# Centering the values before a chunked recurrence instead of centering its outputs

## The reference, cut to what matters

```
state = state * w + (state @ -kk) (kk * a)^T + v k^T
y_t   = state @ r_t                       # one output per feature of v
mean  = mean(y over the head's 64 features);  var = mean((y - mean)^2)
y     = (y - mean) * rsqrt(var + eps) * gn_w + gn_b
y     = y + sum(r * k * r_k) * v          # the bonus, with v as it came
out   = (y * g) @ w_o
```

## Time and profile before

| | |
|---|---|
| runs | 2466.2, 2463.61, 2459.58 us |
| span of the profiled execution, first to last instruction | 2460.2 us |
| PE, DVE, ACT, POOL busy over the span | 2353.0, 1536.6, 663.3, 480.0 us |
| granted TensorE clock, mean | 0.980 |
| recurrence stage | about 557 to 873 us |

### The profile page before, as it was taken

The page is one execution under the profiler, slowest core; times in us unless marked ns, Lnnn a source line. Parts: engine busy times, 40 slices in busy tenths (PEclk is TensorE's granted clock), DMA queues, the critical chain, the costliest instruction groups (busy, mean ns, idle before and its releaser), DMA issues. The chain is left out here.

```text
span 2460.2 us, 43846 instructions
## 1 busy us (share of the span) xinstructions
PE 2353.0 (96%) x17560; PEld 1924.7 (78%) x17560; DVE 1536.6 (62%) x2155; ACT 663.3 (27%) x1274; POOL 480.0 (20%) x313
## 2 busy tenths in 40 slices
PE   7999998997988899999999999999999999999999
PEld 5888886784666678888888888888778887888887
DVE  6656567845777756556576564647766665655654
ACT  3101015535556531010023310102544552200001
POOL 3202131001111133121230221213221112212211
PEclk9999999998999999999999999999988999999999
DMA  4333333431010033333265243333300003233322
GB/s 140 99 89 102 95 94 90 143 112 58 30 30 27 4 103 94 104 93 103 77 197 141 84 121 93 97 92 100 80 1 14 15 1 92 85 106 90 105 83 73
DMA packets 371393, 206.53 MB, mean 84 GB/s; under 512 B 18400, under 2 KB 360352, under 8 KB 371232
## 3 DMA queue, kind: packets, MB, share of 16 engines
q1 hardware_dynamic: 364752, 192.11, 27.5%
q10 hardware_dynamic: 6480, 12.13, 1.4%
HBM read 192.61 MB, written 11.60 MB: 83 GB/s over the span
## 5 line engine op out<-in xcount | busy, mean ns | idle before, releaser
L162 PE MATMUL bank_b<-hhi_b,w_hi_b 128*128 128x512 f32 x872 | 345.6, 396 | 0.0
L164 PE MATMUL bank_b<-hhi_b,w_lo_b 128*128 128x512 f32 x872 | 339.5, 389 | 0.0
L163 PE MATMUL bank_b<-hlo_b,w_hi_b 128*128 128x512 f32 x872 | 339.3, 389 | 0.0
L151 DVE TENSOR_TENSOR w_lo_b<-w_raw,w_hi_b 128x1024 fp32r<-128x1024 f32 (+1 forms) x162 | 287.8, 1776 | 5.6
L162 PE MATMUL bank_a<-hhi_a,w_hi_a 128*128 128x512 f32 x480 | 188.7, 393 | 7.8 <-DVE hlo_a L582 7.8
L163 PEld LDWEIGHTS bank_b<-hlo_b,w_hi_b 128*128 128x128 f32 x872 | 163.7, 188 | 36.8 <-issue 3.4
L162 PEld LDWEIGHTS bank_b<-hhi_b,w_hi_b 128*128 128x128 f32 x872 | 163.7, 188 | 36.6 <-issue 3.4
L164 PEld LDWEIGHTS bank_b<-hhi_b,w_lo_b 128*128 128x128 f32 x872 | 163.7, 188 | 34.5
L163 PE MATMUL bank_a<-hlo_a,w_hi_a 128*128 128x512 f32 x480 | 187.8, 391 | 0.0
L164 PE MATMUL bank_a<-hhi_a,w_lo_a 128*128 128x512 f32 x480 | 187.5, 391 | 0.0
L467 ACT ACTIVATE gated_b<-gsc_b 128x512 f32<-128x512 f32 x44 | 27.9, 634 | 495.2 <-DVE gsc_b L378 495.1
(11 more groups left out here) (404 smaller groups left out, 4918.7 us busy)
## 6 DMA issues: line engine op xcount, KB each, us to landing
w_raw<-in_ffn_w_gate_dram SPq DMA_DIRECT2D x88, 512.0 KB, 3.9
w_raw<-in_ffn_w_up_dram SPq DMA_DIRECT2D x88, 512.0 KB, 3.9
w_raw<-in_ffn_w_down_dram SPq DMA_DIRECT2D x64, 512.0 KB, 3.8
w_raw<-in_ffn_w_down_dram SPq DMA_DIRECT2D x32, 384.0 KB, 3.2
w_raw<-in_rw_w_rkv_dram SPq DMA_DIRECT2D x24, 512.0 KB, 3.7
w_raw<-in_kv_w_dram SPq DMA_DIRECT2D x12, 512.0 KB, 4.7
w_raw<-in_rw_w_o_dram SPq DMA_DIRECT2D x8, 512.0 KB, 6.1
w_raw<-in_nsa_w_q_dram SPq DMA_DIRECT2D x8, 512.0 KB, 3.8
```

The lines of the kernel that those rows point to most:

```text
L151: nc.vector.tensor_tensor(lo, raw, fp(hi), ALU.subtract).then_inc(s["w_ready"], 1)
L162: nc.tensor.matmul(out, whi, hi, start=first, stop=False)
L163: nc.tensor.matmul(out, whi, lo, start=False, stop=False)
L164: return nc.tensor.matmul(out, wlo, hi, start=False, stop=last)
```

## The change

The matrix `center` moves to the front. `values(p)` multiplies v by `center` while turning it, so that `vtok` holds centered values and every output comes out centered. The product `centered` on PE and the copy to `dev` on ACT go. The squares are taken from `ysb` in SBUF, and the normalization reads `ysb`. Since `ysb` now lives until the normalization, it has three buffers (of the same total size as the two `dev` rows and the one `ysb` before), and its writer waits for the normalization three pairs earlier. For pair 0, `values` waits for the constants. The variance no longer waits for the copy.

```diff
@@ buffers
-        ysb, sqy = core.sq[:, 0], [core.sq[:, 1], row("sqy")[:]]
+        ysb, sqy = [core.sq[:, 0], row("ysb1")[:], row("ysb2")[:]], [core.sq[:, 1], row("sqy")[:]]
-        dev, yn = [row(f"dev{n}") for n in range(2)], row("yn")
+        yn = row("yn")
@@ PE
             def values(p):
                 at(pe, p, "lv", 16)
                 at(pe, p - 1, "tok", 3)
+                if p == 0:
+                    pe.wait_ge(s["consts"], 80)
                 for t in range(NT):
-                    m = nc.tensor.transpose(bank[:, TB, t * P:(t + 1) * P], v[:, t * P:(t + 1) * P], core.ident[:])
+                    m = mm(bank[:, TB, t * P:(t + 1) * P], v[:, t * P:(t + 1) * P], center[:], start=True, stop=True)
...
             def variance(p):
                 if 0 <= p < ND:
                     at(pe, p, "sqy", 1)
-                    at(pe, p, "dev", 1)
...
-            def centered(p):
-                if 0 <= p < ND:
-                    at(pe, p, "yadd", 1)
-                    mm(bank[:, EB], center[:], ysb, start=True, stop=True).then_inc(s["cen"], 1)
...
                 m.then_inc(s["f_mm"], 1)
-                centered(p - 1)
                 at(pe, p + 1, "vtok", 1)
...
             output_part(0, 1)
-            centered(last)
             output_part(1, 0)
@@ ACT
-                A(by_parity(ysb), parity_banks(slice(DB, TB + 1), HALF), ACT.Copy).then_inc(s["ysb"], 1)
+                at(act, p - 3, "yn", 1)
+                A(by_parity(ysb[p % 3]), parity_banks(slice(DB, TB + 1), HALF), ACT.Copy).then_inc(s["ysb"], 1)
             def squares(p):
                 if 0 <= p < ND:
-                    at(act, p, "cen", 1)
+                    at(act, p, "yadd", 1)
                     at(act, p - 2, "yn", 1)
-                    A(sqy[p % 2], bank[:, EB], ACT.Square).then_inc(s["sqy"], 1)
-                    A(dev[p % 2][:], bank[:, EB], ACT.Copy).then_inc(s["dev"], 1)
+                    A(sqy[p % 2], ysb[p % 3], ACT.Square).then_inc(s["sqy"], 1)
@@ DVE
-                    TT(ysb[:, C:], bank[:, EB, C:], ysb[:, C:], ALU.add).then_inc(s["yadd"], 1)
+                    y = ysb[p % 3]
+                    TT(y[:, C:], bank[:, EB, C:], y[:, C:], ALU.add).then_inc(s["yadd"], 1)
             def normalized(p):
-                    at(dve, p, "dev", 1)
-                    V.scalar_tensor_tensor(out=yn[:], in0=dev[p % 2][:], scalar=pv[:, p, GNW:GNW + 1], in1=rs[p % 2], op0=ALU.mult,
+                    V.scalar_tensor_tensor(out=yn[:], in0=ysb[p % 3], scalar=pv[:, p, GNW:GNW + 1], in1=rs[p % 2], op0=ALU.mult,
```

More of the change, by code:

```diff
@@ L687 @@
     "rp_mm": 1, "rp": 1, "f_mm": 1, "f": 1, "z_mm": 1, "z": 1, "within": 1, "ysb": 1,
-    "chain": 6, "state": 6, "y_mm": 1, "yadd": 1, "cen": 1, "sqy": 1, "dev": 1, "var": 1, "lny": 1, "rs": 1,
+    "chain": 6, "state": 6, "y_mm": 1, "yadd": 1, "sqy": 1, "var": 1, "lny": 1, "rs": 1,
     "yn": 2, "gated": 1, "yhi": 1, "pair": 1,
```

## The result

The changed kernel took 2468.24 us, the median of 20 runs (2463.24 to 2471.79). The kernel before took 2464.51 us, the median of 20 (2458.77 to 2469.23). The ratio is 1.0016, with a 95% interval of 1.0009 to 1.0023: slower by 3.7 us, or 0.16%. The forecast was 0.6 us faster. The time lies in the range, the sign is wrong.

What follows compares the result with a forecast made beforehand. No engine fills a recurrence step; it is a loop of short waits between PE, DVE and ACT. Terms of -0.6 and +0.04, about -0.6, gave 2460.2 - 0.6 + 3.4 = 2463.0 us; range 2457 to 2469.5.

Steps and rivals of the forecast that it cites:

- The centering product on PE: Removing the 1.06 us product from seven recurrence steps wins 0.6 us, with ends of nothing and 2.0 us.
- the three pairs: Pairs 2, 3 and 7, where PE is late: at most 0.45, 0.45 and 1.06 us won, 0.2 taken at each.
- its being 1.06 earlier gives nothing: In pairs 1, 4 and 5 PE's product already waits when DVE's L1430 starts, so removing the centering product wins nothing.
- L1430's successor should again start unheld: Check in pairs 1, 4, 5 and 6: DVE's work there starts right after bt, without waiting for PE.
- pair 7's place: No bt follows there, so up to the whole 1.06 us of the removed product can be won; 0.2 taken.
- The 3.4 us put on the span: The median run, 2463.6 us, lies 3.4 above the profiled span, so 3.4 is added to the sum.
- The values: Turning v by products on PE takes 1.12 us instead of the transposes' 0.66, 0.46 more per pair, hidden except 0.04.
- The cover: PE's 0.79 us idle behind the values, waiting for DVE's state, hides the dearer turn up to 1.45 us.
- ACT and the end: Dropping ACT's 0.6 us copy per pair and moving the squares wins nothing; after the last pair, DVE, POOL and ACT decide.
- Instructions late more often: Slower rival, chance 0.15: PE runs out of instructions in more pairs; two more steps at 3.1 us give 2469.2 us.
- Full yield: Faster rival, chance 0.20: the full 2.0 us come, 2461.6 us, or 2457.1 if the long steps are mended too.
- the outgrown product: Slower rival, chance 0.05: the turning products exceed 1.45 us; at 3.3 us they cost 13 us, giving 2476 us.

Runs made afterwards that it cites:

- shifts of 64 and 128: 16 or 32 small unread products (64 or 128 PE instructions) before pair 0's bonus; changed kernel 0.9975, again 0.9991, and 0.9983; kernel before 0.9998 and 0.9997.
- the middle shift: The changed kernel with 16 small unread products in pair 4's step, ahead of pair 5's bonus product: 2459.51 us, 0.9987 of the kernel before.
- the cut programs: Six programs, both kernels and variants, cut off behind the recurrence stage, later stages left out; kernel before 883.85 us, changed 885.71 us.

## Why the prediction was wrong

*The centering product on PE, the step that failed.* The prediction bounded the gain at 2.0 us and took 0.6, since "the pause grows and the gain is nil". That reading of the pauses was right for the three pairs: they grew by 1.1, 0.8 and 1.2 us. What it left out: it looked only at the pauses that were there. Pauses of 1.2 to 1.9 us also opened in pairs 1, 4, 5 and 6, which had none, and in pairs 4, 5 and 6 they reach past bt. The step that failed is therefore "its being 1.06 earlier gives nothing", with nothing as the lower end of the term; it had to lie below nothing. Measured: 7.4 us of product gone, 11.1 us of "issue" come in the first pair of profiles and 6.6 in the mean of all. The removal by itself gave 1.0013 [1.0005, 1.0022], where the term had promised a gain, and the product put back cost nothing. The pauses so explain why nothing was won. That the kernel came out slower is a second thing, and it hangs on where the borders fall: the stage's 4.7 us appear at the unshifted places and not at the shifts of 64 and 128, as far as single profiles tell. The prediction had taken the shift of the borders for a small gain, 0.2 us at each of three places; its size and its sign were open.

*"L1430's successor should again start unheld" in pairs 1, 4, 5 and 6.* Wrong in all four: L1424 is held for 0.13, 0.81, 0.34 and 0.71 us. Only in pair 1 does the pause end in time for the scores, as bt's end at 646.63 decides.

*The last two steps.* The prediction gave pair 7's place a gain of up to 1.06 us. Instead its pause grew from 0.19 to 1.38 us (before 853.00), more than the product had taken, and these steps grew by 3.4 us: there are also the pauses before 820.87 and in L893, three in the update products L924, and a granted clock of 0.97 where it was 1.00. Which of these carries how much was not separated. The growth is no accident of one execution (67.34 and 66.27 us in the two others of this stage), and the middle shift takes it away.

*The 3.4 us put on the span.* In each kernel run here the profiled execution took 1.8 us more than its span (2468.05 against 2466.25 us for the changed one). So 1.8 of the 3.4 are around a run, and the other 1.6 only say that the profiled execution of the kernel before was a quick one. The forecast of the median is not touched by it.

*The values.* Eight products of two records took the forecast time, and the wait behind them shrank:

```profile
704.49 1.16 PE L859 MATMUL bank_rec<-center_rec,v_rec 128*128 128x128 f32 x8
705.93 0.33 PE L996 MATMUL bank_rec<-st_rec,ft_rec 64*64 64x64 f32 x4 [0.29 <-DVE st_rec L1432]
...
PE bank_rec L996 <- DVE st_rec L1432: 8.3, 20, 0.9
```

1.16 us against 1.12 forecast, 0.29 idle against "about 0.3"; L996 waits 8.3 us in all, where L1001 had waited 10.7. The cover held, and the turn alone cost nothing that can be told (1.0003). The rule that the prediction quotes from the Trainium skill's "Perfetto Trace Analysis", section "Transposes", would have been no reason against this edit.

*ACT and the end.* Right: ACT's 3.9 us less bought nothing. At the end ACT is held by POOL as before, against the earlier trace rows; the last variance is there 2.0 us ahead of ACT's split (866.28 against 868.32), where the two had met, and that head start bought nothing either:

```profile
865.26 1.02 PE L900 MATMUL bank_rec<-sqy_rec,head_ones 128*128 128x512 f32 x2
...
868.32 0.63 ACT L1192 ACTIVATE y_hi<-yn_rec 128x512 fp32r<-128x512 f32 x1 [3.89 <-POOL yn_rec L1275]
```

*The rivals.* "Instructions late more often" was right, and had 0.15. Its price of 3.1 us a step was too high: many pauses of 0.5 to 1.9 us came instead of a few of 2.3, mostly beside DVE's work, and only a part reached the loop. The range held the measured time because this rival had set its upper end; the sum itself had the wrong sign. "Full yield" and the outgrown product did not happen.

*What stays open.* In the stage the change costs 1.9 us by the times of the cut programs, and 2.9, 4.6 and 6.7 us by three pairs of profiled executions; so between half and all of the 3.7 us is made there. Whether anything beyond it comes from the attention's clock, and why the odds of that clock follow what PE did a thousand microseconds earlier, was not settled. Nor is it known which pauses make an unlucky place of the borders unlucky. That the pauses are waits for instruction blocks rests on their places, on the block transfers ahead of each of them (next section) and on how they move with the stream; no run changed the fetching itself.

## What to carry to other kernels

Where a profile shows "issue" inside groups of equal small products, and block transfers of the instruction queue end shortly ahead of each pause, the engine may be running at the pace at which its instructions arrive, as here: work taken off it turned into longer and more frequent pauses, also at places that had shown none. Price such a removal with zero in the middle of the range, not at its end. Compare a change of a few microseconds there with one that only shifts the stream by some useless products, since 16 of them alone moved the changed kernel by more than the change did (2459.51 against 2468.24 us, or 0.9987 against 1.0016 of the kernel before, in the middle of the stage). Compare several places of both kernels, not one of each; and repeat the best of several such variants before believing it.

## What the runs showed of the hardware

PE's pauses with "issue" follow the transfers of its instruction blocks. In the kernel before, one block of instructions moved in the 1.1 us from 715.4 to 716.5, in the midst of the 2.28 us before 717.81; in the changed kernel one did so between 748.7 and 749.8, ahead of the products that go on at 751.12. First the former, then the latter (packets, MB, share):

```profile
q8 instruction: 1, 0.02, 5.5%
```

```profile
q8 instruction: 1, 0.02, 5.3%
```

Some 1.3 us after each of these stretches ends, PE goes on. The same holds for every pause of this kind: in the 20 profiled executions PE has 236 pauses of 0.4 us and more with "issue" in the stage, and each ends 1.0 to 1.6 us after the end of a block's transfer, while the 543 waits of that length for other engines lie spread, nine in ten of them from 0.4 to 5.9 us after one. (The first such pause of the stage, at 577 us, is left out: no block had moved for 30 us in most of them.) The transfers last 0.9 to 1.6 us, and no two of them start less than 3.2 us apart, with some 250 of PE's records between two starts at the median. By these figures PE waits where it would go through such a block's records in less time.

The Trainium skill's "Runtime: NRT & Kernel Launch", section "Instruction fetch mechanics", says that the cost of crossing a block's border is mostly hidden. In this stage the trace disagrees: 9.6 us of "issue" in 290 us before, 20.7 in 294 after.

A product of 128x128 in 32-bit floats takes 0.275 us for each of its two records, as much as one transpose (0.273), so four turns cost 1.16 us and not 0.66.
